# Earlier loads for attention, and a shorter selection for one tile, in a one-core streaming step

## The chip, the cores and the metric

One core of a Trainium2 chip runs the whole kernel as one launch. The metric is the time of an execution on the device, in microseconds; less is better. The engines are TensorE (PE; its weight loads are shown as PEld), VectorE (DVE), ScalarE (ACT), GpSimd (POOL) and SyncE (SP), which here only issues DMAs.

## The reference, cut to what matters

A layer takes 1024 prompt tokens, 64 sample tokens and 16 meta tokens of width 1024. After a norm one projection gives queries, keys, values and gates. Two mixers run beside each other: A is a sliding window with a sink in its softmax, B attends to the best 256 keys of an indexer's scores. Their gated sum goes through w_o and an MLP.

```python
rel = relu(einsum('bqhd,bsd->bqhs', qi, ki))
score = einsum('bqh,bqhs->bqs', wi, rel) * INDEX_SCALE
score = where(admissible[None], score, -inf)
top_val, top_idx = lax.top_k(score, n_sel)          # n_sel = 256
...
s = where(valid, s - slopes * dist, -inf)           # B, over the keys kept
p = softmax(concatenate([s, sm], -1)); out = p @ v  # sm: scores of the meta keys
...
mix = (sigmoid(g_a) * o_a + sigmoid(g_b) * o_b) @ w_o
```

## The kernel before

Everything is float32; each product is made from a rounded part ("hi") and a remainder ("lo"). The kernel is a row of blocks. Inside a block each engine runs its own list of instructions, tied by semaphores; a block ends when all engines have ended theirs, and only then does the next begin. DMAs are issued in program order by the engine whose list they stand in.

**projection** goes through the columns of w_in in chunks 1 to 9 (chunk 0 is done with the norm). Chunks 1 to 5 give queries, feature-major in 12 groups; 6 to 9 give gates, in 9 groups of token tiles (the last of 64 rows). A group is 24 matmuls in one PSUM bank (L894). ScalarE evacuates it to `stage` (`evacuate`, L635), SyncE stores it (`store`, L523; three stage slots). Between the groups of chunks 1 to 5, 7 and 8, TensorE makes the index scores of one of seven tiles, ScalarE their relu and weighting (L672, L676), GpSimd the sum over heads (`add_head`, L740), and VectorE selects (L865, L869): a round finds the eight largest of each row and overwrites them with TAKEN, 32 rounds for 256 keys, two tiles interleaved. `finish` turns the scores into a mask of distances. The last tile in this order is tile 2, with 384 keys; its first 20 rounds run beside the last 20 of tile 3 with 512 keys.

In the last chunk, SyncE waits until all index scores are added and loads the attention keys in natural order, twice each (`load_keys`, 12 prompt DMAs, 16 for the sample part), then goes on with the stores. After groups 0 to 6 TensorE turns three key groups each (`turn_attention_keys`, L917; 21 in all, 11 of them of the prompt); ScalarE copies each twice (L654, L655), GpSimd makes the lo parts (`keys_lo`, L759). When TensorE has ended its last group, GpSimd zeroes the sink rows and sets the ones columns of the values (L775, L778), and SyncE loads the first section's queries (L600), all values (L607) and stores the last four masks (L545), then waits for its stores, and the block ends. The raw keys, the index keys and the projection's weights lie where values, queries and keys are put later, which is why such loads wait.

**attention** has 18 sections: tiles 7 to 0 and then the sample tile, branch A and then B of each. A section has 16 units (two halves, 8 pairs of heads; 8 for the sample). A unit is `score` (L1504), `subtract_distance` on VectorE (L1439), `exp` on ScalarE (L1397), `turn` (L1518), copies (L1391, L1451), `weigh_values` (L1534). Section 0's queries are split by ScalarE (L1405) and VectorE (L1472) at the block's start, all later ones by GpSimd, one section ahead (`split_queries`, L1346, L1349). SyncE's list is: load_q(1), wait for the masks, distances, gates, copies to the outputs, then the loads and stores of each section. After attention come w_o with the norms, and the MLP.

## Time and profile before

| | us |
|---|---|
| runs, median of 3 (lowest to highest) | 2042.55 (2040.95 to 2051.41) |
| the profiled execution, its own time | 2042.43 |
| its span, first to last instruction | 2040.6 |
| TensorE matmul busy (share) | 1924.3 (94%) |
| VectorE busy | 1178.2 (58%) |
| ScalarE busy | 713.2 (35%) |
| GpSimd busy | 578.8 (28%) |

Times in the rows are from the start of the span. Chunk 9 of the projection runs from 521 to 587 us, attention from 613.6 to about 1070 us. PEclk is the granted clock as a share of 2.4 GHz, so 0.50 is 1.2 GHz. "Idle before" is the time in which the engine stood, and the arrow says for whom.

### The profile page before, as it was taken

What the parts mean: (1) busy time and instruction counts of PE and PEld (TensorE: products, weight loads), DVE (VectorE), ACT (ScalarE), POOL (GpSimd) and SP (SyncE); (2) the same over time, 40 slices, a digit from 0 to 9 for tenths busy, and PEclk for the clock granted to TensorE, in tenths of its full rate; (3) what the DMA queues carried; (4) which work ended last, traced back from release to release, by engine and by line L of the source; (5) the groups of instructions that cost most, each with busy time, mean ns of one, the idle gap of its engine ahead of it and who ended that gap; (6) DMA issues with size and microseconds to landing.
All of it is one profiled execution on the core that took longest, in us unless ns stands there. A gap on an engine that the chain in (4) does not pass through costs nothing. (4 is left out here: it accounts for less than half of the span.)

```text
span 2040.6 us, 31131 instructions
## 1 busy us (share of the span) xinstructions
PE 1924.3 (94%) x11132; PEld 1734.4 (85%) x11132; DVE 1178.2 (58%) x2701; ACT 713.2 (35%) x1421; POOL 578.8 (28%) x444
## 2 busy tenths in 40 slices
PE   5989999999849999999997989999999999999995
PEld 5879999877638999999996868888888888888884
DVE  5249999998746566666754653333333333333337
ACT  4335544233215555655544332112122121212122
POOL 2315554133213232445611002222222222222224
PEclk9999999999977999999978999999999999999998
DMA  5423333332349134444613312111111111111104
GB/s 166 130 71 85 93 95 88 94 106 80 81 92 185 39 70 89 95 92 93 122 38 115 138 57 93 42 41 41 41 46 41 42 45 41 46 41 46 54 8 154
DMA packets 147465, 160.18 MB, mean 78 GB/s; under 512 B 35776, under 2 KB 115504, under 8 KB 147360
## 3 DMA queue, kind: packets, MB, share of 16 engines
q1 hardware_dynamic: 136416, 141.10, 26.0%
q10 hardware_dynamic: 10944, 17.72, 3.7%
q8 instruction: 62, 1.02, 0.2%
q14 instruction: 43, 0.35, 0.1%
HBM read 120.63 MB, written 39.27 MB: 78 GB/s over the span
## 5 line engine op out<-in xcount | busy, mean ns | idle before, releaser
L2042 PE MATMUL ps<-x2T_hi,weights 128*128 128x362 f32 (+1 forms) x1536 | 383.8, 329 | 5.3 <-DVE weights L2008 5.3
L2060 PE MATMUL ps<-weights,hid_hi 128*128 128x512 f32 (+1 forms) x1152 | 363.0, 396 | 0.0
L2042 PEld LDWEIGHTS ps<-x2T_hi,weights 128*128 128x128 f32 x1536 | 273.9, 189 | 7.0 <-DVE weights L2008 5.5
L1993 DVE TENSOR_TENSOR total<-total,ps 128x512 f32<-128x512 f32 (+1 forms) x270 | 184.9, 687 | 164.2 <-PE ps L2060 163.3
L2060 PEld LDWEIGHTS ps<-weights,hid_hi 128*128 128x128 f32 (+1 forms) x1152 | 209.6, 182 | 57.1
L2042 PE MATMUL ps<-x2T_lo,weights 128*128 128x362 f32 (+1 forms) x768 | 253.1, 330 | 0.0
L1978 DVE TENSOR_TENSOR hidden<-hidden 128x362 f32<-128x362 f32 (+1 forms) x96 | 51.6, 537 | 311.6 <-ACT hidden L1951 311.6
L2060 PE MATMUL ps<-weights,hid_lo 128*128 128x512 f32 (+1 forms) x576 | 228.1, 396 | 0.0
L869 DVE MATCH_REPLACE8 score<-top,score 128x1024 f32<-128x1024 f32 (+6 forms) x224 | 207.2, 930 | 0.0
L865 DVE MAX8 top<-score 128x8 f32<-128x1024 f32 (+6 forms) x224 | 203.1, 937 | 1.9
L1911 POOL TENSOR_TENSOR weights<-down_raw,weights 128x512 fp32r<-128x512 f32 x64 | 83.0, 1296 | 419.6 <-ACT weights L1942 419.6
L1397 ACT ACTIVATE probs<-probs,neg 128x209 f32<-128x209 f32 (+19 forms) x272 | 168.9, 622 | 12.7 <-DVE neg L1439 10.7
L1534 PE MATMUL ps<-v_b_p,pt 128*128 128x65 f32 (+2 forms) x1280 | 172.7, 278 | 0.0
L1391 ACT ACTIVATE pt<-ps 128x512 f32<-128x512 f32 (+3 forms) x224 | 104.7, 490 | 194.1 <-PE ps L1518 193.8
L1534 PEld LDWEIGHTS ps<-v_b_p,pt 128*128 128x128 f32 (+2 forms) x1280 | 166.4, 195 | 5.7
L1903 POOL TENSOR_TENSOR weights<-up_raw,weights 128x256 fp32r<-128x256 f32 x124 | 87.9, 749 | 289.8 <-ACT weights L1933 289.8
L1518 PE MATMUL ps<-ident,probs 128*128 128x128 f32 (+2 forms) x976 | 164.1, 287 | 0.6 <-ACT probs L1397 0.6
L894 PE MATMUL ps<-xT_hi,w_hi 128*128 128x362 f32 (+1 forms) x480 | 159.4, 332 | 1.6 <-PEq L160 1.6
L894 PE MATMUL ps<-xT_hi,w_lo 128*128 128x362 f32 (+1 forms) x480 | 158.2, 330 | 0.0
L894 PE MATMUL ps<-xT_lo,w_hi 128*128 128x362 f32 (+1 forms) x480 | 157.9, 329 | 0.0
L1942 ACT ACTIVATE weights<-down_raw 128x512 fp32r<-128x512 f32 x64 | 40.1, 626 | 317.6 <-PE ps L2060 317.5
L1951 ACT ACTIVATE hidden<-ps 128x362 f32<-128x362 f32 (+1 forms) x96 | 45.5, 474 | 288.4 <-PE ps L2042 288.4
(188 smaller groups left out, 3618.6 us busy)
## 6 DMA issues: line engine op xcount, KB each, us to landing
w_raw<-in_w_in ACTq DMA_DIRECT2D x64, 256.0 KB, 3.0
up_raw<-in_w_up SPq DMA_DIRECT2D x64, 256.0 KB, 2.8
down_raw<-in_w_down SPq DMA_DIRECT2D x64, 256.0 KB, 2.6
q_raw<-q_scr SPq DMA_DIRECT2D x30, 512.0 KB, 8.1
gates<-gate_scr SPq DMA_DIRECT2D x34, 256.0 KB, 4.7
x_in<-in_x_prompt SPq DMA_DIRECT2D x16, 512.0 KB, 4.7
gate_scr<-stage SPq DMA_DIRECT2D x32, 256.0 KB, 3.1
q_scr<-stage SPq DMA_DIRECT2D x40, 181.0 KB, 3.0
```

Of the source, the lines that this page charges most:

```text
L865: dve.max(top8[:tile_rows(INDEX_TILES[i]), i % 2], works[i]).then_inc(select_step[i % 2], 1)
L869: dve.match_replace(works[i], top8[:tile_rows(INDEX_TILES[i]), i % 2], works[i], TAKEN)\
L894: last = pe.matmul(out, a, b, start=(k == 0 and j == 0), stop=(k == KT - 1 and j == 2))
L1391: act.activation(pt[:, u % PT, a:a + n, :], src, ACT.Copy).then_inc(copied_act, 1)
L1397: act.activation(probs[:, u % 3, 0:w], probs[:, u % 3, 0:w], ACT.Exp, bias=neg[:, branch, h:h + 1], scale=-1.0).then_inc(exped, 1)
L1518: last = pe.transpose(ps[0:rows, T_BANK + x % 3, b * P:(b + 1) * P], probs[:, u % 3, col:col + rows], c["ident"][:])
L1534: last = pe.matmul(out_bank(q)[:, a, :], pt[0:rows, u % PT, j, :], values(u, j, rows), start=(j == 0), stop=(j == len(tiles) - 1))
L1903: pool.tensor_tensor(up_lo[:, k, :], up_raw[:, k // 2, k % 2, :], up_hi[:, k, :].bitcast(F32), ALU.subtract).then_inc(up_lo_done, 1)
L1911: pool.tensor_tensor(down_lo[at], down_raw[:, u, :], down_hi[at].bitcast(F32), ALU.subtract).then_inc(down_lo_done, 1)
L1993: dve.tensor_tensor(out, out, ps[:r, UP_BANKS + g % DOWN_BANKS, :], ALU.add).then_inc(added, 1)
L2042: last = pe.matmul(ps[:, g % UP_BANKS, 0:n], a[:, k, fs], b, start=(k == 0 and i == 0), stop=(k == KT - 1 and i == 2))
L2060: last = pe.matmul(ps[:r, UP_BANKS + g % DOWN_BANKS, :], a, b[:, f, cols], start=(f == 0 and i == 0), stop=(f == FT - 1 and i == 2))
```

## The change

- **Last chunk, loads.** SyncE loads only the prompt's keys (`load_prompt_keys`, 9 DMAs; the meta rows are written twice by one DMA) and behind them the first section's queries (`load_first_queries`, 2 DMAs). The sample part moves to ScalarE's queue behind its evacuation of group 0 (`load_sample_keys`, 10 DMAs).
- **Last chunk, keys.** TensorE turns none after group 0, four key groups after each of groups 1 to 5 and the last after group 6.
- **Values.** Only branch A's prompt values are loaded in the last chunk, in two parts after the stores of groups 6 and 7, once GpSimd has zeroed their sink rows, for which it waits until all keys are turned. The meta rows of blocks three apart are one DMA, so 15 DMAs stand for 26. Branch B's values are loaded in the attention block and waited for at section 1, the sample's at the sample tile; the fills for them move there too.
- **First queries.** They get a place of their own (`q_st_first`); ScalarE rounds them after evacuating group 7, GpSimd subtracts at the end of its list. The splitting at the start of attention goes.
- **Masks.** The last four are stored at the start of attention, ahead of B's values; load_q(1) then waits until they have landed, since its buffer lies over theirs.
- **Selection of tile 2.** `by_removal`: 384 keys less 256 leaves 128, fewer than 256, so GpSimd sums the negated scores in reversed order of keys, VectorE finds the 128 largest in 16 rounds, and `finish` masks those taken instead of those not taken.
- **Places.** Weights, keys, queries and attention's buffers are laid out anew; `half_of` gives hi and lo parts of a chunk the same half.

```diff
-W_RAW_AT = FOOT + 4 * HALF + X_BYTES
+KEYS_FROM = FOOT + X_BYTES + 2 * HALF
+W_RAW_AT = FOOT + X_BYTES + 4 * HALF
+Q_RAW_AT = W_RAW_AT + 4 * RAW * 512
...
+    out = place(nc, *first, FOOT, ("xT_hi", [P, KT, N_TOK], F32R), ("xT_lo", [P, KT, N_TOK], F32R), ("w", [P, 4, KT, 512], F32R),
...
+    return place(nc, KEYS_FROM, *[(n + "_fp32", shape, F32) for n, shape in KEYS])
...
+    return place(nc, ("q_st_first", [P, 2, HEADS, CHUNK], F32R), ("v_a_p", [P, SAMPLE_BLOCK, 2, 2 * COL], F32),
+                 ("v_a_s", [P, 2, 2 * COL], F32), ("v_b_p", [P, 9, COL], F32), ("v_b_s", [P, 9, COL], F32),
+                 FOOT, ("wo_raw", [P, KT, D], F32), ("pt", [P, PT, 9, P], F32), ("probs", [P, 3, N_META + N_QUERY], F32),
+                 ("merged", [P, 2, D // 2], F32),
+                 FOOT + X_BYTES, ("gates", [P, 2, 2, D // 2], F32), ("mixed", [P, 2, 2, D // 2], F32),
+                 ("q_st3", [P, 2, 2, HEADS, CHUNK], F32R), KEYS_FROM, *[(n, shape, F32R) for n, shape in KEYS],
+                 Q_RAW_AT, ("q_raw3", [P, 2, HEADS, P], F32), ("dist_b", [P, 2, N_META + N_QUERY], F32),
+                 ("neg", [P, 2, 2 * PAIRS], F32), ("neg_part", [P, 2, 2], F32), ("inv", [P, 2, QUAD], F32))
...
+    ROWS, ONES = sink_rows(kv, sample=False), ones_columns(kv, "v_a_p")
+    A_VALUES = banded_values(kv, t_scr)
+    q_first, q_first_hi = sem("p3_q_first"), sem("p3_q_first_hi")
+    FIRST_QUERIES = split_places(kv["q_st_first"], kv["q_raw3"][:, 0], 2)
+    VALUES_AT = 6
+    REVERSED_AT = 512
+    KEY_COLS = [slice(T_KA, T_KA + HD), slice(T_KA + HD, T_KA + 2 * HD), slice(T_KB, T_KB + HD)]
...
-        return range(min(3 * g, len(GROUPS)), min(3 * g + 3, len(GROUPS)))
-
+        first = max(0, 4 * (g - 1))
+        return range(min(first, len(GROUPS)), min(4 * g, len(GROUPS)))
...
+    def by_removal(i):
+
+
+        return keys_seen(INDEX_TILES[i]) - TOPK < TOPK
+
+    def work_place(i):
+        at = REVERSED_AT if by_removal(i) else N_META
+        return score[:tile_rows(INDEX_TILES[i]), mask_slot(i + 2), at:at + keys_seen(INDEX_TILES[i])]
...
-            def load_keys():
-                new, meta = slice(N_PROMPT, N_QUERY), slice(N_QUERY, N_TOK)
-                cols = [slice(T_KA, T_KA + HD), slice(T_KA + HD, T_KA + 2 * HD), slice(T_KB, T_KB + HD)]
...
+            def load_prompt_keys():
+                for i, cols in enumerate(KEY_COLS):
+                    src = t_scr[0:N_PROMPT, cols].rearrange("(j p) d -> p j d", p=P)
+                    for half in range(2):
+                        sp.dma_start(raw["raw_p"][:, :, i, half], src).then_inc(prompt_loaded, 16)
+                    src = t_scr[N_QUERY:N_TOK, cols]
+                    sp.dma_start(raw["raw_m"][:, i], src.unsqueeze(1).to_broadcast([N_META, 2, HD])).then_inc(prompt_loaded, 16)
+
+            def load_first_queries():
+                t = ATTENTION_ORDER[0]
+                src = q_scr[0:D, t * P:(t + 1) * P].rearrange("(h d) n -> d h n", d=HD)
                 for half in range(2):
-                    for i in range(3):
-                        sp.dma_start(raw["raw_p"][:, :, i, half, :], t_scr[0:N_PROMPT, cols[i]].rearrange("(j p) d -> p j d", p=P))\
-                          .then_inc(prompt_loaded, 16)
-                        sp.dma_start(raw["raw_m"][:, i, half, :], t_scr[meta, cols[i]]).then_inc(prompt_loaded, 16)
-                for half in range(2):
-                    for i in range(3):
-                        sp.dma_start(raw["raw_n"][:, i, half, :], t_scr[new, cols[i]]).then_inc(sample_loaded, 16)
-                        sp.dma_start(raw["raw_cm"][:, i, half, :], cache_meta[0, 0, :, (0, 1, 4)[i], :]).then_inc(sample_loaded, 16)
-                    sp.dma_start(raw["raw_ca"][:, :, half, :], cache_k_a[0, 0]).then_inc(sample_loaded, 16)
-                    sp.dma_start(raw["raw_cb"][:, :, half, :], cache_k_b[0, 0, :, 0, :].rearrange("(j p) d -> p j d", p=P))\
-                      .then_inc(sample_loaded, 16)
+                    sp.dma_start(kv["q_raw3"][half * HD:(half + 1) * HD, 0], src).then_inc(q_first, 16)
+
+            def load_values(part):
+                for dst, src in A_VALUES[part::2]:
+                    sp.dma_start(dst, src).then_inc(values_loaded, 16)
 
...
             for ch in range(1, N_CH):
                 if ch == LAST:
                     sp.wait_ge(added, IDX_HEADS * len(INDEX_TILES))
-                    load_keys()
+                    load_prompt_keys()
+                    load_first_queries()
                 for g in range(len(groups_of(ch))):
                     store(ch, g)
+                    if ch == LAST and g == VALUES_AT:
+                        sp.wait_ge(value_rows_set, len(ROWS))
+                        load_values(0)
+                    if ch == LAST and g == VALUES_AT + 1:
+                        load_values(1)
                     if ch == INDEX_CHUNK and g == 3:
                         for u in range(GROUP_BASE[ch] + 4 - STAGE, GROUP_BASE[ch] + 4):
...
                     store_mask(i + 2, INDEX_TILES[i])
-            def load_first_queries(heads, loaded):
-                t = ATTENTION_ORDER[0]
-                src = q_scr[heads.start * HD:heads.stop * HD, t * P:(t + 1) * P].rearrange("(h d) n -> d h n", d=HD)
-                for half in range(2):
-                    sp.dma_start(kv["q_raw3"][half * HD:(half + 1) * HD, 0, heads, :], src).then_inc(loaded, 16)
-
-            sp.wait_ge(group_done, GROUP_BASE[N_CH])
-            for piece in range(2):
-                load_first_queries(slice(8 * piece, 8 * piece + 8), kv["q_first"][piece])
-            sp.wait_ge(value_rows_set, VALUE_SETS)
-            for dst, src in value_loads(kv, t_scr, cache_v_a, cache_v_b, cache_meta):
-                sp.dma_start(dst, src).then_inc(values_loaded, 16)
-            for i in LATE_MASKS:
-                store_mask(i + 2, INDEX_TILES[i])
             all_stored(N_CH - 1)
...
                 hi.then_inc(kt_hi_done, 1)
                 as_is.then_inc(kt_raw_done, 1)
 
+            def load_sample_keys():
+                act.wait_ge(added, IDX_HEADS * len(INDEX_TILES))
+                for i, cols in enumerate(KEY_COLS):
+                    src = t_scr[N_PROMPT:N_QUERY, cols]
+                    act.dma_start(raw["raw_n"][:, i], src.unsqueeze(1).to_broadcast([N_SAMPLE, 2, HD])).then_inc(sample_loaded, 16)
+                    src = cache_meta[0, 0, :, (0, 1, 4)[i], :]
+                    act.dma_start(raw["raw_cm"][:, i], src.unsqueeze(1).to_broadcast([N_META, 2, HD])).then_inc(sample_loaded, 16)
+                for half in range(2):
+                    act.dma_start(raw["raw_ca"][:, :, half], cache_k_a[0, 0]).then_inc(sample_loaded, 16)
+                    act.dma_start(raw["raw_cb"][:, :, half], cache_k_b[0, 0, :, 0, :].rearrange("(j p) d -> p j d", p=P))\
+                       .then_inc(sample_loaded, 16)
+
+            def first_queries_hi():
+                act.wait_ge(q_first, 32)
+                act.wait_ge(kt_turned, PROMPT_GROUPS)
+                st, loaded = FIRST_QUERIES(slice(0, P))
+                act.activation(st, loaded, ACT.Copy).then_inc(q_first_hi, 1)
+
             def queries_hi(i):
                 r = tile_rows(INDEX_TILES[i])
                 act.wait_ge(q_loaded, 32 * (i + 1))
...
+                    if ch == LAST and g == 0:
+                        load_sample_keys()
                     if ch == LAST:
                         for j in key_groups_at(g):
                             copy_keys(j)
+                    if ch == LAST and g == VALUES_AT + 1:
+                        first_queries_hi()
                     if ch == INDEX_CHUNK and g == QUERIES_AT:
                         queries_hi(0)
...
-                out = score[:r, mask_slot(i + 2), N_META:N_META + n]
-                if h == 0:
+                out = work_place(i)
+                if h:
+                    pool.wait_ge(added, v)
+                else:
                     slot_free(pool, i + 2)
+                if by_removal(i):
+                    back = rel[:r, v % 2, n - 1::-1]
+                    if h == 0:
+                        pool.tensor_scalar(out, back, -1.0, None, ALU.mult).then_inc(added, 1)
+                    else:
+                        pool.tensor_tensor(out, out, back, ALU.subtract).then_inc(added, 1)
+                elif h == 0:
                     pool.tensor_copy(out, rel[:r, v % 2, 0:n]).then_inc(added, 1)
                 else:
-                    pool.wait_ge(added, v)
                     pool.tensor_tensor(out, out, rel[:r, v % 2, 0:n], ALU.add).then_inc(added, 1)
...
             pool.wait_ge(kt_lo_done, 3)
+            pool.wait_ge(kt_lo_done, 3)
+            pool.wait_ge(kt_turned, len(GROUPS))
+            for rows in ROWS:
+                pool.memset(rows, 0.0).then_inc(value_rows_set, 1)
+            pool.wait_ge(value_rows_set, len(ROWS))
+            for col in ONES:
...
             pool.wait_ge(kt_lo_done, 6)
-            pool.wait_ge(group_done, GROUP_BASE[N_CH])
-            for rows in sink_rows(kv):
-                pool.memset(rows, 0.0).then_inc(value_rows_set, 1)
-            pool.wait_ge(value_rows_set, len(sink_rows(kv)))
-            for col in ones_columns(kv):
-                pool.memset(col, 1.0).then_inc(value_rows_set, 1)
+            pool.wait_ge(q_first_hi, 1)
+            st, loaded = FIRST_QUERIES(slice(HD, P))
...
-                    dve.memset(score[0:CHUNK, slot, N_META + n - CHUNK:N_META + n], UNSEEN).then_inc(select_step[i % 2], 1)
+                    if by_removal(i):
+                        dve.memset(score[0:CHUNK, slot, REVERSED_AT:REVERSED_AT + CHUNK], -UNSEEN).then_inc(select_step[i % 2], 1)
+                    else:
+                        dve.memset(score[0:CHUNK, slot, N_META + n - CHUNK:N_META + n], UNSEEN).then_inc(select_step[i % 2], 1)
...
-                dve.tensor_scalar(work, work, TAKEN, -FAR, ALU.not_equal, ALU.mult).then_inc(select_step[i % 2], 1)
+                mask = score[:r, mask_slot(i + 2), N_META:N_META + n]
+                if by_removal(i):
+                    dve.tensor_scalar(mask, work[:, n - 1::-1], TAKEN, -FAR, ALU.is_equal, ALU.mult).then_inc(select_step[i % 2], 1)
+                else:
+                    dve.tensor_scalar(mask, work, TAKEN, -FAR, ALU.not_equal, ALU.mult).then_inc(select_step[i % 2], 1)
...
+            rounds = [(keys_seen(t) - TOPK if by_removal(i) else TOPK) // 8 for i, t in enumerate(INDEX_TILES)]
+            first = [0, rounds[0], rounds[0] + 12]
...
-                pe.wait_ge(sample_loaded if group.sample else prompt_loaded, 16 * (16 if group.sample else 12))
+                pe.wait_ge(sample_loaded if group.sample else prompt_loaded, 16 * (10 if group.sample else 9))
...
+def split_places(st, loaded, blocks):
+
+
+    return lambda rows: (st[rows, 0:blocks].rearrange("p e h n -> p h e n"),
+                         loaded[rows, :, 0:blocks * CHUNK].rearrange("p h (e n) -> p h e n", n=CHUNK))
+
+
+def banded_values(kv, t_scr):
+
+
+    va, out = kv["v_a_p"], []
+    cols_a, meta = slice(T_VA, T_VA + 2 * HD), slice(N_QUERY, N_TOK)
...
-        for i in range(blocks[1]):
-            tile, row = divmod(col, P)
-            out.append((va[row:row + N_META, blocks[0] + 3 * i, tile, VALUES], t_scr[meta, cols_a]))
+        (first, count), (tile, row) = blocks, divmod(col, P)
+        src = t_scr[meta, cols_a].unsqueeze(1).to_broadcast([N_META, count, 2 * HD])
+        out.append((va[row:row + N_META, first:first + 3 * count - 2:3, tile, VALUES], src))
...
+                for n in range(MASKS - SCORES, MASKS):
+                    t = INDEX_TILES[n - 2]
+                    w = N_META + keys_seen(t)
+                    sp.dma_start(dist_scr[t, 0:tile_rows(t), 0:w], kv["score"][:tile_rows(t), mask_slot(n), 0:w])\
+                      .then_inc(mask_stored[mask_slot(n)], 16)
+                for dst, src in B_VALUES:
+                    sp.dma_start(dst, src).then_inc(b_values_loaded, 16)
+                for n in range(MASKS - SCORES, MASKS):
+                    sp.wait_ge(mask_stored[mask_slot(n)], 16 * (n // SCORES + 1))
                 load_q(1)
-                for n in range(MASKS - SCORES, MASKS):
-                    sp.wait_ge(kv["mask_stored"][mask_slot(n)], 16 * (n // SCORES + 1))
                 for i in range(2):
                     load_dist(i)
                 for i in range(2):
                     load_gates(i)
+                sp.wait_ge(late_rows_set, len(LATE_SETS))
+                for dst, src in SAMPLE_VALUES:
+                    sp.dma_start(dst, src).then_inc(s_values_loaded, 16)
...
 
+                for n, (dst, value) in enumerate(LATE_SETS):
+                    if n:
+                        pool.wait_ge(late_rows_set, n)
+                    pool.memset(dst, value).then_inc(late_rows_set, 1)
...
-                        pe.wait_ge(kv["values_loaded"], 16 * VALUE_LOADS)
+                        pe.wait_ge(kv["values_loaded"], 16 * A_VALUES)
+                    if u == SECTION_END[0]:
+                        pe.wait_ge(late_rows_set, len(LATE_SETS))
+                        pe.wait_ge(b_values_loaded, 16 * len(B_VALUES))
+                    if u == SAMPLE_FROM:
+                        pe.wait_ge(s_values_loaded, 16 * len(SAMPLE_VALUES))
                     if act_copies(GROUPS[u + 1]):
```

## Rows read from the trace of the kernel before

**Rows 1.** The page, part 2: granted TensorE clock in 40 slices of 51 us, in tenths.

```profile
PEclk9999999999977999999978999999999999999998
```

**Rows 2.** Waits from 515 to 640 us: waiter, released by, us in total, times, longest.

```profile
PE ps L1504 <- DVE q_st L1472: 29.7, 1, 29.7
...
PE ps L917 <- DMA raw_m<-t_scr: 6.8, 1, 6.8
```

**Rows 3.** Stretches: us, PE, PEld, DVE, ACT, POOL busy (x), PEclk, DMA share, GB/s.

```profile
534.50:537.40 2.90, 2.90 (x10) 2.36 (x9) 2.90 (x8) 1.60 (x4) 0.00 (x0) 0.51 0.29 66
...
615.90:638.50 22.60, 21.90 (x108) 21.65 (x109) 13.57 (x60) 10.19 (x24) 6.43 (x2) 0.50 0.91 186
...
900.00:1000.00 100.00, 100.00 (x845) 96.20 (x844) 72.73 (x285) 59.78 (x125) 48.53 (x24) 1.00 0.59 105
...
588.00:589.00 1.00, 0.00 (x0) 0.00 (x0) 0.00 (x0) 0.00 (x0) 0.94 (x4) 0.76 0.55 133
```

**Rows 4.** TensorE in time: start us, us, engine, line, op, out<-in, count, idle before.

```profile
526.09 0.40 PE L894 MATMUL ps<-w_hi,xT_lo 128*128 128x512 f32 x1
533.31 0.28 PE L917 MATMUL ps<-ident,raw_m 16*128 16x16 f32 x1 [6.83 <-DMA raw_m<-t_scr]
```

**Rows 5.** SyncE's DMA issues in time: start us, us, what, count.

```profile
523.34 0.36 SPq L565 DMA_DIRECT2D raw_p<-t_scr  x1
...
530.11 0.81 SPq L567 DMA_DIRECT2D raw_m<-t_scr  x1
...
586.92 0.63 SPq L523 DMA_DIRECT2D gate_scr<-stage  x1
587.60 2.66 SPq L600 DMA_DIRECT2D q_raw<-q_scr  x4
590.30 13.62 SPq L607 DMA_DIRECT2D v_a_p<-t_scr  x26
...
610.62 2.42 SPq L545 DMA_DIRECT2D dist_scr<-score  x4
613.59 1.42 SPq L1266 DMA_DIRECT2D q_raw<-q_scr  x2
```

**Rows 6.** DMA issues from 515 to 640 us: count, KB each, median us to landing.

```profile
q_raw<-q_scr SPq DMA_DIRECT2D x5, 512.0 KB, 7.7
...
q_raw<-q_scr SPq DMA_DIRECT2D x4, 256.0 KB, 5.0
...
gate_scr<-stage SPq DMA_DIRECT2D x2, 128.0 KB, 2.4
...
dist_scr<-score SPq DMA_DIRECT2D x1, 200.0 KB, 3.1
```

**Rows 7.** ScalarE and GpSimd in time, around the seam.

```profile
580.77 0.60 ACT L635 ACTIVATE stage<-ps 128x512 f32<-128x512 f32 x1 [4.04 <-PE ps L894]
586.31 0.59 ACT L635 ACTIVATE stage<-ps 64x512 f32<-64x512 f32 x1 [4.94 <-PE ps L894]
...
613.60 2.00 ACT L1405 ACTIVATE q_st<-q_raw 128x1024 fp32r<-128x1024 f32 x2 [26.70 <-PEq L511]
...
586.40 2.32 POOL L775 MEMSET v_a_p<- 32x128 f32 x3 [5.51 <-PE ps L894]
...
622.15 1.89 POOL L1346 CAST q_st<-q_raw 128x2048 fp32r<-128x2048 f32 x1 [32.88 <-DMA q_raw<-q_scr]
624.12 4.54 POOL L1349 TENSOR_TENSOR q_st<-q_raw,q_st 64x2048 fp32r<-64x2048 f32 x1
```

**Rows 8.** TensorE's score matmuls in time: section 0's first, section 1's first, two in section 2.

```profile
615.97 1.61 PE L1504 MATMUL ps<-k_a_p,q_st 128*128 128x208 f32 x6 [29.69 <-DVE q_st L1472]
...
638.57 1.66 PE L1504 MATMUL ps<-k_b_p,q_st 128*128 128x488 f32 x4
...
704.63 0.46 PE L1504 MATMUL ps<-k_a_p,q_st 128*128 128x208 f32 x2
...
713.27 0.46 PE L1504 MATMUL ps<-k_a_p,q_st 128*128 128x208 f32 x2
```

**Rows 9.** VectorE in time: the last rounds of the selection.

```profile
569.24 0.56 DVE L865 MAX8 top<-score 128x8 f32<-128x384 f32 x1
...
584.24 0.36 DVE L843 TENSOR_SCALAR score<-score 128x384 f32<-128x384 f32 x1
584.64 0.56 DVE L847 TENSOR_TENSOR score<-score,dist 128x384 f32<-128x384 f32 x1
```

135 lines of the change are left out of this document (57 added, 78 removed).

## The prediction

> **What bounds the kernel now.** I read the page's clock line first, then who TensorE waited for, then stretches of time around the two long waits, and last the queues of SyncE and of the other engines there. TensorE is busy nearly everywhere and the granted clock is full for most of the span [rows 1]; what is left are holes. The list of waits names the largest: 29.7 us at L1504 for the first queries, and 6.8 us at L917 for the prompt keys' meta rows [rows 2]. Both lie at the seam between projection and attention. The stretches [rows 3] show what the holes cost besides themselves: after the first the clock is at 1.2 GHz (0.51) while chunk 9 restarts; after the second it is at 1.2 GHz for the whole first section of attention, 615.9 to 638.5 us, although TensorE is busy for 21.9 of these 22.6 us. From 640 to 1000 us TensorE never idles and has the full clock (the last 100 of these are in [rows 3]; the stretches before read alike), so a microsecond gained ahead of section 1 (the second section, tile 7 branch B) is a microsecond of the end; nothing behind it has an absolute time.
>
> The first hole: SyncE begins to load keys at 523.34, when the index scores are added, and issues twelve DMAs until 530.9 [rows 5]; TensorE has ended group 0 of chunk 9 at about 526.5 and stands until 533.31 [rows 4]. The second: TensorE's last group ends near 586.3. SyncE then issues the last gate store, 4 query loads, 37 value loads and 4 masks one after the other, from 586.92 to 613.04, and the next block opens at 613.59 [rows 5]. Then come the rounding and subtraction of the queries before TensorE starts at 615.97 [rows 7, 8]. So the issue of 45 small DMAs is the bound of that hole, not their bytes.
>
> **Part 1, keys a group later, fewer DMAs.** SyncE issues 9 prompt DMAs instead of 12, without the 12 short raw_n/raw_cm and 4 raw_ca/raw_cb loads behind them (they go to ScalarE's queue as 10). TensorE turns no key after group 0 but does group 1 first. A group is 24 matmuls or 5.54 us (the last two evacuations start 5.54 us apart, 580.77 and 586.31, [rows 7]), so the keys are wanted at 532.0 instead of 526.5. Old landing: 533.3. New: twelve issues took 7.6 us (523.34 to 530.92, [rows 5]), 0.63 each, so the ninth begins near 528.4, and with the old issue-to-landing of 3.2 us (533.31 less 530.11, [rows 4, 5]) that is 531.6 if issue is the limit. The same bytes must come, though: if the DMA engines are the limit, only the issue of later loads goes away, and 533.3 stays. So the remaining stall is 0 to 1.3 us; I take 0.3, nearer the issue limit. The removed idle is 6.83 us [rows 4]; the work from 533.31 to 537.4 at half clock would shrink by between 1.3 us (if transposes gain little) and half of 4.1, which is 2.05; I take 1.6. Sum: -6.8 - 1.6 + 0.3 = -8.1 us; the last evacuation starts at 578.2 instead of 586.3. The ScalarE issues (10 at the same 0.63 us, from 527.1 to about 533.4) come ahead of its copies of groups 0 to 3; TensorE wants these copies back only at group 2's end, 539, with some 2 us to spare.
>
> **Part 2, the shorter selection.** Alone, this is needed for part 1 to count. VectorE now ends at 585.2, just ahead of TensorE; twelve rounds of the 384-key tile run alone from 569.24 to 584.24, 1.25 us each [rows 9]. With 16 rounds instead of 32, started at the same time, these twelve vanish (-15.0 us) and four of the shared rounds lose this tile's half (about -0.9 us each, -3.6; an estimate from the same 1.25 less the idle that the other tile's instructions then no longer fill). VectorE ends near 567. Without it the block could not end before 585.2, and some 4 us of the gain would stay behind. It buys nothing more. GpSimd's eight additions read backwards: forwards they take 1.0 us and wait 4 us each for ScalarE; no row shows a backward read. Below: no gain, as they are covered by that wait; above: twice the time, which puts the last one, the keys' gate, 1 us later. I take 0 and keep 1 us.
>
> **Part 3, the block's end.** After group 6 the last key is turned (near 567); GpSimd sets the zero rows, 2.32 us [rows 7]; SyncE issues 8 value loads at 13.62/26 = 0.52 us [rows 5], ending near 573.4, the store of group 7, then 7 loads, ending near 577.7. That is ahead of the last evacuation's end (578.8). The merged meta copies make 15 of 26. The last store is issued at 578.8 and lands about 2.4 us later [rows 6], at 581.2; with the 0.55 us between blocks (613.04 to 613.59) attention opens at 581.75. ScalarE rounds the first queries behind evacuation 7, 2.0 us, and GpSimd subtracts in 4.54 us [rows 7], from near 575.3 to 579.8: hidden by 1.4 us. If that cover is gone, each microsecond counts whole. TensorE starts at once, since the 2.4 us of rounding and subtraction in the block are gone: 581.9 instead of 615.97. That is -34.1 us so far: 8.1 from part 1, 26.0 from here.
>
> **Part 4, section 0 and its successor.** What is late next is load_q(1). It now sits behind 4 mask stores (2.42 us), 4 value loads (2.1 us) and the wait for the masks' landing (3.1 us after the last issue), since its buffer shares their place: it is issued at about +5.0 and +5.7 us from the block's opening instead of +0. With 7.7 us to landing [rows 6] it is there at +13.4; with 5 us (four 256 KB query loads took that, [rows 6]) at +10.7. GpSimd's cast and subtraction, 1.89 + 4.54 us [rows 7], end at +17.2 to +20. Section 1 is wanted at +0.15 + 22.6 us if section 0 runs as slowly as now [rows 8]: covered by 3 us. The distances, issued until +9 and landing within 9 us, are covered too. So whether section 0 is faster decides. The hole is now 578.2 to 581.9, 3.7 us. In the present trace the clock fell 2.2 us after the last matmul (the stretch from 588 to 589 us averages 0.76, [rows 3]), so a hole of 3.7 us probably takes it down again, and section 0's own work did not bring it back in 22.6 us. I take 22.6 unchanged.
>
> The Trainium skill (TensorE: Matmul & The Clock Gate, "What's actually happening") says that the throttle is the default state and that recent activity of TensorE releases it. By that rule a section that keeps TensorE busy would soon run at full clock; this trace speaks against it for this work, since 21.9 busy microseconds of 22.6 left it at half.
>
> **Sum.** The profiled execution took 2042.43 us (2.0 us around its span of 2040.6), and the median of the runs is 2042.55, the same. Parts 1 and 3 give -34.1; part 2 and part 4 nothing. 2042.4 - 34.1 = 2008.3; I say 2008.
>
> **Rivals.** (a) The clock survives the short hole, chance 0.12. Units of section 0 then come every 0.864 us (ten from 704.63 to 713.27, [rows 8]), the section would be done at +13.5, and load_q(1) becomes the bound, at +17.2 to +20: 2.8 to 5.6 us less, of which a new idle of some 5 us gives back 1 in a cold start. 2003 to 2006. (b) The seam has a new last one: prompt keys still at 533.3 or later, with the clock dropped again (2 to 6 us), or GpSimd's chain, or SyncE's 15 value loads, running past the last store. For: three covers of 1 to 2 us each in a row. Against: each is made of durations shown. Chance 0.22, 2010 to 2016. (c) The value loads or queries are needed sooner than they land, so that the hole moves into attention: load_q(1) later than +22.6. It would take 3 us more than the 7.7 us of landing; the queue is emptier than it was. Chance 0.05, 2010 to 2014. (d) Slower than before: GpSimd reads backwards far slower. In chunk 8 it has per head 5.5 us less 1.3 (w_lo) less 1.0, so 3.2 us of room; beyond it each head holds up ScalarE's next relu and TensorE's index scores. Eight heads must lose over 34 us in all, thus an addition of about 8.5 us instead of 1.0, before the gain is gone. Nothing in the trace shows such a price. Chance 0.02, 2045. The forecast has the remaining 0.59.
>
> **Range.** Forecast alone: 2005 to 2011 (0.3 to 1.3 us of key stall, 1 us of backward reads, the phase at which the clock falls and rises, about 1.7 us each way). With (a) and most of (b): 2003 to 2015. A measurement of this kernel can tell about 0.5%, 10 us, from no change. Faster by more: every case but (d) and a far tail of (b) and (c), 0.96; within: 0.02; slower: 0.02.
>
> **What the new profile would show.** TensorE's wait at L917's successor is gone or under 1.5 us and no clock of 0.5 near 530; VectorE's last selection ends before 570; the hole at the seam is 3.5 to 4.5 us; the first value product does not wait for values; section 0 lasts 22 us at 0.50 (right) or 17 to 20 with a wait for q_st at its end (rival a); from section 1 on all lies 34 us earlier. I am wrong if the seam's last wait is GpSimd's or if the clock there is full.

## The result, and the profile after

The changed kernel took 2018.56 us, median of four runs (2012.18, 2018.38, 2018.73, 2020.75); the kernel before, timed beside it, took 2046.98 (2040.95, 2042.55, 2051.41, 2051.59; the median falls between two pairs). The ratio is 0.986, 95% interval 0.982 to 0.990. It is faster by more than the 0.5% that can be told, but 10 us slower than the 2008 that I predicted, and outside my range of 2003 to 2015. The profiled execution took 2018.38 us, span 2016.6.

The page's clock line of the changed kernel, which answers to [rows 1]. One slice at the seam still reads 7 (before, two slices did), and the dip at the end of attention, 7 and 8 from 1020 us before, now reads 6, 8 and 8 from 958 us:

```profile
PEclk9999999999979999999688989999999999999998
```

The waits of the changed kernel from 515 to 640 us, answering to [rows 2]: the wait of 29.7 us is 3.9 us for the block's opening, the wait for the keys 2.3:

```profile
PE ps L1577 <- PEq L530: 3.9, 1, 3.9
...
PE ps L970 <- DMA raw_m<-t_scr: 2.3, 1, 2.3
```

Stretches of the changed kernel (columns as in [rows 3]): group 1 and the wait for keys, the turning behind it, the seam, sections 0 and 1, then sections 13, 14, 15 and 16:

```profile
526.50:534.10 7.60, 5.30 (x24) 3.95 (x22) 7.60 (x22) 0.97 (x2) 0.00 (x0) 1.00 0.97 210
534.10:536.40 2.30, 2.30 (x15) 2.05 (x16) 2.30 (x7) 2.04 (x9) 0.00 (x0) 1.00 1.13 257
579.60:583.40 3.80, 0.00 (x0) 0.03 (x1) 0.00 (x1) 0.58 (x2) 1.86 (x2) 1.00 0.65 123
583.40:605.50 22.10, 21.28 (x108) 21.03 (x109) 12.52 (x59) 10.36 (x24) 7.01 (x7) 0.52 0.97 226
605.50:659.10 53.60, 53.60 (x419) 51.73 (x419) 34.54 (x101) 28.37 (x40) 11.75 (x6) 0.98 0.51 100
949.90:966.70 16.80, 16.80 (x146) 15.95 (x144) 12.65 (x51) 11.13 (x26) 9.43 (x5) 1.00 0.69 139
966.70:987.80 21.10, 21.01 (x118) 19.03 (x115) 12.52 (x65) 8.30 (x25) 12.01 (x8) 0.65 0.49 108
987.80:1011.20 23.40, 23.40 (x106) 20.91 (x105) 10.06 (x48) 7.97 (x24) 5.92 (x4) 0.50 0.22 45
```

The same three last sections in the kernel before, which no row ahead of the prediction shows (sections 13, 14, 15):

```profile
982.10:998.90 16.80, 16.80 (x145) 15.95 (x144) 12.57 (x51) 11.12 (x26) 9.70 (x5) 1.00 0.87 138
998.90:1013.90 15.00, 14.68 (x118) 13.27 (x115) 11.60 (x64) 8.09 (x25) 11.24 (x7) 1.00 0.28 66
1013.90:1033.80 19.90, 19.90 (x107) 17.92 (x105) 10.07 (x50) 8.19 (x25) 6.46 (x6) 0.62 0.58 117
```

The reader is to see two things. First, section 13 is alike to the tenth, and section 14 (tile 0, branch A) is not: 15.0 us at full clock before, 21.1 at 0.65 after, with the same 118 matmuls. Second, the time of the whole is made of these two places. Read by the start of each section:

| first score matmul of | before | after | moved |
|---|---|---|---|
| section 0 | 615.97 | 583.40 | -32.6 |
| section 1 | 638.57 | 605.54 | -33.0 |
| section 14 | 998.91 | 966.68 | -32.2 |
| section 15 | 1013.89 | 987.78 | -26.1 |
| section 16 | 1033.78 | 1011.23 | -22.6 |
| end of the span | 2040.6 | 2016.6 | -24.0 |

So 32 us of the promised 34.1 arrive at section 14. Then 9.6 us are given back in sections 14 and 15, whose work the change leaves as it was, and 1.4 us return behind attention. In the trace the half clock holds from 1018.6 for 30.7 us before, from 973.2 for 54.6 us after.

How the seam came about. SyncE's issues in the changed kernel, answering to [rows 5]:

```profile
523.10 0.99 SPq L583 DMA_DIRECT2D raw_p<-t_scr  x2
...
525.11 2.54 SPq L583 DMA_DIRECT2D raw_p<-t_scr  x2
...
529.69 1.52 SPq L585 DMA_DIRECT2D raw_m<-t_scr  x1
...
570.72 3.99 SPq L595 DMA_DIRECT2D v_a_p<-t_scr  x8
...
575.23 4.12 SPq L595 DMA_DIRECT2D v_a_p<-t_scr  x7
580.17 0.63 SPq L542 DMA_DIRECT2D gate_scr<-stage  x1
583.37 2.20 SPq L1363 DMA_DIRECT2D dist_scr<-score  x4
585.60 2.71 SPq L1366 DMA_DIRECT2D v_b_p<-t_scr  x4
588.87 1.31 SPq L1335 DMA_DIRECT2D q_raw<-q_scr  x2
```

TensorE at the three places of [rows 4, 8]:

```profile
534.10 0.23 PE L970 MATMUL ps<-ident,raw_m 16*128 16x16 f32 x1 [2.30 <-DMA raw_m<-t_scr]
...
583.40 0.97 PE L1577 MATMUL ps<-k_a_p,q_st_first 128*128 128x208 f32 x6 [3.88 <-PEq L530]
...
605.54 1.97 PE L1577 MATMUL ps<-k_b_p,q_st 128*128 128x488 f32 x4
```

GpSimd in the changed kernel, answering to [rows 7], with one of the additions of tile 2 that read backwards, and VectorE's last mask, answering to [rows 9]:

```profile
511.15 1.01 POOL L779 TENSOR_TENSOR score<-score,rel 128x384 f32<-128x384 f32 x1
...
576.84 4.58 POOL L825 TENSOR_TENSOR q_st_first<-q_raw,q_st_first 64x2048 fp32r<-64x2048 f32 x1 [1.93 <-ACT q_st_first L688]
...
596.39 1.89 POOL L1425 CAST q_st<-q_raw 128x2048 fp32r<-128x2048 f32 x1 [12.17 <-DMA q_raw<-q_scr]
598.36 4.53 POOL L1428 TENSOR_TENSOR q_st<-q_raw,q_st 64x2048 fp32r<-64x2048 f32 x1
```

```profile
566.48 0.69 DVE L900 TENSOR_TENSOR score<-score,dist 128x512 f32<-128x512 f32 x1
```

### The profile page after: what moved, and what is told of

Read it like the earlier page. It is cut to its first block and busy times, and to the rows that moved or that the text cites. A ratio compares the mean times of both kernels' runs of the same rounds, so it can differ in the third digit from the quotient of the medians.

```text
span 2016.6 us, 31063 instructions
## 1 busy us (share of the span) xinstructions
PE 1930.6 (96%) x11132; PEld 1740.3 (86%) x11132; DVE 1160.4 (58%) x2651; ACT 712.6 (35%) x1420; POOL 584.8 (29%) x445
## 5 line engine op out<-in xcount | busy, mean ns | idle before, releaser
L947 PE MATMUL ps<-xT_hi,w 128*128 128x362 f32 (+1 forms) x960 | 245.9, 330 | 1.6 <-PEq L160 1.6
L922 DVE MATCH_REPLACE8 score<-top,score 128x1024 f32<-128x1024 f32 (+5 forms) x208 | 199.2, 965 | 0.0
L918 DVE MAX8 top<-score 128x8 f32<-128x1024 f32 (+5 forms) x208 | 195.0, 971 | 1.6
L947 PE MATMUL ps<-w,xT_hi 128*128 128x512 f32 (+1 forms) x576 | 180.8, 395 | 0.0
L947 PEld LDWEIGHTS ps<-xT_hi,w 128*128 128x128 f32 x960 | 171.6, 189 | 2.5 <-POOL w L208 2.0
L947 PE MATMUL ps<-xT_lo,w 128*128 128x362 f32 (+1 forms) x480 | 157.7, 329 | 0.0
```

The costliest lines, as they stand in the source:

```text
L918: dve.max(top8[:tile_rows(INDEX_TILES[i]), i % 2], works[i]).then_inc(select_step[i % 2], 1)
L922: dve.match_replace(works[i], top8[:tile_rows(INDEX_TILES[i]), i % 2], works[i], TAKEN)\
L947: last = pe.matmul(out, a, b, start=(k == 0 and j == 0), stop=(k == KT - 1 and j == 2))
```

## Experiments

**Theories.** A: the change is worth what its seam shows, 32 to 33 us; the rest of the miss is the clock falling at another moment among the small sections 14 to 17, which changes from run to run in either kernel. B: the change itself makes those sections slower (other places in memory, loads moved into attention), so the loss belongs to it.

### Both kernels again

No edit. Kernel before:

> The kernel before, unchanged, timed five times more. Theory A (the clock in the last small sections of attention falls at a moment that differs from execution to execution, in either kernel): the times spread over 5 to 10 us, and within the kernel the longer ones have the lower mean granted clock; in its profile, TensorE's scores of section 1 begin near 638.6 us as before, but the fall of the clock after 900 us need not be at 1018.6. Theory B (the new kernel's layout or loads make the clock fall earlier): the old kernel falls at about 1018 us every time, and its times lie within 0.3%.

Twelve runs: three at 2041.40 to 2042.46 and nine at 2049.77 to 2054.29, nothing between (ratio 1.002, 1.000 to 1.004). The runs of the kernel before beside it lie the same way, 12 of 23 at 2040 to 2043 and 11 at 2051 to 2054. This profile, of 2053.16 us, is one of the long ones; its sections 13 and 14:

```profile
981.90:998.70 16.80, 16.80 (x145) 15.95 (x144) 12.55 (x51) 11.10 (x26) 9.71 (x5) 1.00 0.91 149
998.70:1022.50 23.80, 23.80 (x118) 21.64 (x115) 12.68 (x65) 8.21 (x25) 11.72 (x8) 0.56 0.57 115
```

Up to 998.7 it is the profile before to 0.3 us; then section 14 takes 23.8 us instead of 15.0, because the half clock begins at 1001.4 (61.4 us long) instead of 1018.6 (30.7). The same program thus has two lengths 10 us apart, by when the clock falls; the three shorter runs have a mean granted clock of 0.964 to 0.965, the nine longer ones 0.957 to 0.959. I call them short and long runs. That shows A's mechanism without any change, and the profile that I had taken my sum from was one of the short kind.

> The changed kernel, unchanged. Theory A: times spread from about 2008 to 2021 us; where the clock falls as late as the old kernel's did, the time is near 2009; all spans up to section 14 (tile 0, branch A) repeat within 1 us of 966.7 for its first score. Theory B: it falls near 974 us every time and all times lie near 2018.

2012.35, and five of 2017.41 to 2020.84; ratio 0.986 (0.983 to 0.989). The profile repeats the one above: section 0 at 582.98, section 14 from 966.28 to 987.32, half clock from 972.9 for 54.6 us. Of ten runs of the changed kernel two are short (2012.2 and 2012.4), eight long.

### The selection alone

On the kernel before: `by_removal`, `work_place`, the reversed sums and 16 rounds for tile 2, with nothing else of the change.

```diff
...
-            ROUNDS = TOPK // 8
+            rounds = [(keys_seen(t) - TOPK if by_removal(i) else TOPK) // 8 for i, t in enumerate(INDEX_TILES)]
...
```

> The kernel before with the shorter selection of tile 2 alone. My account: nothing waits for VectorE there, so section 0 still starts at 616.0 +- 0.3 us and section 1 at 638.6; VectorE's last mask ends near 567 instead of 585.2. The rival (VectorE did hold the block's end, or the reversed reads on GpSimd cost) would move section 0's start: earlier by up to 1 us, or later by 1 us or more.

Ten runs of 2049.43 to 2052.84; ratio 1.002 (1.000 to 1.004). VectorE's last mask ends at 568.3 instead of 585.2, and TensorE's waits are what they were:

```profile
PE ps L1528 <- DVE q_st L1496: 29.7, 1, 29.7
PE ps L941 <- DMA raw_m<-t_scr: 7.1, 1, 7.1
```

The edit buys nothing alone, as I had it; section 0 began at 616.47 and section 1 at 639.07, 0.5 us later than in the kernel before, a little outside the 0.3 us that I allowed. Its sections 14 and 15 bear on theory B. The layout and the loads of this kernel are those of the kernel before, and yet the two sections are the changed kernel's, with the clock falling 6.5 us into section 14 and staying down for 54.6 us in both:

```profile
1000.20:1021.30 21.10, 21.02 (x117) 19.03 (x115) 12.49 (x65) 8.29 (x25) 11.69 (x8) 0.65 0.51 112
```

All ten runs are of the long kind, where 15 of 35 runs of the unchanged kernel on the same chip were short: an edit that touches nothing on the path may still weigh on which kind comes up.

### The change without the shorter selection

```diff
-        return keys_seen(INDEX_TILES[i]) - TOPK < TOPK
+        return False
```

> The changed kernel with 32 rounds for tile 2 again. My account: VectorE ends at about 585, so that the attention block opens at 585.5 to 586 instead of 583.4, section 0 starts 2 to 2.5 us later than in the changed kernel, and that is all the shorter selection is worth here. Rival: the selection carries much of the gain (10 us or more lost without it).

2007.90 to 2023.27, median 2020.03; ratio 0.988 (0.984 to 0.992). The profile, of the fastest run, shows what it holds back: VectorE ends at 584.58 and the block opens at 584.86 instead of 583.37, so 1.5 us, not the 4 that I had (nor the 2 to 2.5 expected here). In this run the clock happened to rise early in section 0, and TensorE then met the next limit:

```profile
584.90:603.90 19.00, 14.58 (x108) 14.03 (x108) 12.66 (x61) 10.90 (x24) 6.96 (x7) 0.85 0.95 235
```

```profile
PE ps L1577 <- POOL q_st L1428: 4.2, 1, 4.2
```

GpSimd's subtraction of section 1's queries ended at +19.0 us, and section 1 began there. This is my rival (a), by chance of the clock.

### The keys turned as before

```diff
-        first = max(0, 4 * (g - 1))
-        return range(min(first, len(GROUPS)), min(4 * g, len(GROUPS)))
+        return range(min(3 * g, len(GROUPS)), min(3 * g + 3, len(GROUPS)))
```

> The changed kernel, but three key groups turned after each of groups 0 to 6 as before, with the new loads. My account of part 1: the prompt keys land near 534 whoever waits, so TensorE now stands from 526.2 to 534 (about 7.8 us instead of 2.3), the clock falls in it and costs 1 to 2 us more, and section 0 starts 5.5 to 7.5 us later than the changed kernel's 583.4. Rival (the fewer DMAs did it, not the later turning): the hole stays near 2 us and section 0 starts within 1 us of 583.4.

2016.04 and three of 2024.93 to 2025.77; ratio 0.988 (0.984 to 0.992). The wait is back, and with it the half clock (530.3, 6.8 us), and section 0 begins at 590.41, 7.0 us later than with the change:

```profile
PE ps L969 <- DMA raw_m<-t_scr: 7.7, 1, 7.7
```

So turning a group later is worth 7.0 us of the 32.6. The keys land near 534 (533.73 and 534.10) whether TensorE waits from 526.05 or from 531.8, and they landed at 533.31 in the kernel before: nine DMAs instead of twelve, now with ten loads of the sample part beside them from ScalarE's queue, did not bring them earlier.

### A warm clock through the seam

Behind the last group stand 14 matmuls of 512 columns into a bank that nobody reads, on the changed kernel:

```diff
+            pe.wait_ge(kt_hi_done, len(GROUPS))
+            pe.wait_ge(kt_raw_done, len(GROUPS))
+            for _ in range(14):
+                pe.matmul(ps[:, 5, :], xT_hi[:, 0, 0:P], w_hi[:, half_of(LAST), 0, :], start=True, stop=True)
```

> The changed kernel with 14 matmuls of 512 columns behind the last group, into a bank that nobody reads, so that TensorE works through 3.2 of the 3.9 us hole. If the clock stays at full level, section 0 needs 13.5 us of work, GpSimd's subtraction for section 1 (done 19.5 us after the block's opening) becomes the bound, and section 1 starts near 603, 2.5 us earlier than the changed kernel's 605.5. If section 0's own work cannot hold the clock, it falls within the section and section 1 starts between 603 and 605.5.

Ratio 0.986 (0.983 to 0.990), as without it. The clock held through the seam, and section 0, which began at 585.04 instead of 583.40, was done 13 us after its start, but section 1 began at 604.78 instead of 605.54:

```profile
585.00:598.00 13.00, 12.06 (x108) 11.71 (x108) 11.64 (x59) 10.26 (x23) 0.63 (x5) 1.00 0.86 221
```

```profile
PE ps L1581 <- POOL q_st L1432: 6.6, 1, 6.6
```

During that wait of 6.6 us the clock fell (600.6, for 10.2 us), and section 1 took 55.3 us instead of 53.6. A fast section 0 is worth nothing while load_q(1) is late: the second half of rival (a), measured.

### load_q(1) earlier, then with the warm clock

Masks 5 and 6 are stored behind the store of group 1 of chunk 9, 7 and 8 behind that of group 6, and load_q(1) stands ahead of B's values:

```diff
+                    if ch == LAST and g == 1:
+                        store_mask(5, INDEX_TILES[3])
+                        store_mask(6, INDEX_TILES[4])
...
+                        sp.wait_ge(mask_ready, MASKS)
+                        store_mask(7, INDEX_TILES[5])
+                        store_mask(8, INDEX_TILES[6])
```

> The changed kernel with the last four masks stored in the last chunk, so that load_q(1) is the first DMA of attention. By my account load_q(1) is covered when section 0 runs at half clock: section 1 still starts near 605.5 us, and only GpSimd's subtraction ends some 5 us earlier, near 598. Rival: load_q(1) holds section 1 already, and section 1 starts earlier by 1 us or more.

2010.21 to 2018.86, median 2016.11; ratio 0.984 (0.981 to 0.988). Section 1 begins at 602.83, 2.7 us sooner and not near 605.5 as expected. That doesn't show that load_q(1) held it before: in this profile the clock fell at 586.25 for only 6.8 us, so that section 0 ran mostly at full clock and lasted 14.9 us. It began late, at 587.97: the wait for the keys was 2.8 us, and half clock from 535.05 for 6.8 us went with it.

> Both together: the 14 matmuls in the hole and the masks stored early. If the clock holds and load_q(1) was the only bound behind it, section 1 starts 14 to 15 us after section 0, near 598, 7 us earlier than the changed kernel; if it does not hold, near 605 as without.

Both edits together. 2001.99 to 2015.65, median 2013.16; ratio 0.982 (0.978 to 0.986). In the profile, of the fastest run, section 1 begins at 598.97, 6.6 us ahead of the changed kernel's, section 14 at 958.98, 7.7 ahead:

```profile
583.90:599.00 15.10, 12.26 (x109) 11.74 (x109) 12.58 (x61) 10.83 (x24) 7.04 (x7) 1.00 0.97 198
```

In this run the clock fell only at 977.27, in section 15, and section 14 took what it takes in the profile before, 15.0 us with 14.68 busy, though the places in memory and, but for the masks and load_q(1), the loads are those of the changed kernel:

```profile
959.00:974.00 15.00, 14.68 (x118) 13.27 (x115) 11.63 (x64) 8.09 (x25) 11.53 (x7) 1.00 0.27 62
```

With the selection-only run this is the plainest evidence against B: section 14 has the short form in the new layout and the long form in the old one. The profiles without the shorter selection (965.39 to 980.37) and of the keys turned from group 2 on (963.35 to 978.33) have the short form too.

### Work that holds the clock in the last sections

On this last variant, in sections 14 to 16, one extra matmul of 252 columns per unit (then two), whose result is never read:

```diff
+                    if ALL[u][0] in range(14, 17):
+                        for _ in range(1):
+                            pe.matmul(ps[:, O_BANK + q % 2, QUAD * COL:512], kv["k_b_p"][:, 0, 0:P], kv["k_b_p"][:, 0, 0:512 - QUAD * COL],
+                                      start=True, stop=True)
```

> The kernel with masks early and the seam filled (the one with 14 matmuls), and in sections 14 to 16 (tile 0 and the sample's branch A, 40 units) one more matmul of 252 columns ahead of each unit's value products, into unused columns of the output bank. If TensorE's sparse work in the small sections lets the clock fall, more work there holds it longer: the half-clock stretch that starts between 973 and 983 us gets shorter or goes, and for 5 to 6 us of added work some 5 to 12 us come back; times near 2000 to 2008 with less spread. Rival (the fall has nothing to do with how dense the work is): the stretch stays 34 to 58 us and the time is about 5 to 9 us longer than without, as the additions run at half clock.

Five runs of 1990.65 to 1995.20 and one of 2020.45, median 1991.56; ratio 0.975 (0.970 to 0.979). More work, and 20 us less time by the medians (10 against the fastest run without it). The expectation was 2000 to 2008. Sections 14 and 15 of the profile:

```profile
960.00:976.10 16.10, 16.03 (x130) 14.65 (x127) 12.06 (x64) 8.23 (x25) 11.67 (x7) 1.00 0.32 74
976.10:991.40 15.30, 15.18 (x122) 13.74 (x121) 9.53 (x49) 7.92 (x25) 5.92 (x5) 1.00 0.66 140
```

> As the one before with two such matmuls per unit: 80 in all, 10 to 12 us of work at full clock. By the density account the half-clock stretch is gone in every execution and the sections 14 to 16 take their full-clock time plus 10 to 12 us: no faster than one matmul per unit, but the narrowest spread. Rival: longer by twice the amount of the one before, stretch unchanged.

Four runs of 1993.53 to 1997.04, median 1995.10; ratio 0.974 (0.971 to 0.976). No run fell back, as one had with a single matmul; the second matmul costs its own time, some 3.5 us.

### Tile 0 elsewhere, and the keys two groups later

Both on the kernel with masks early and a warm seam, without the work in the last sections. First the order of the tiles:

```diff
-ATTENTION_ORDER = list(range(SAMPLE_TILE - 1, -1, -1)) + [SAMPLE_TILE]
+ATTENTION_ORDER = [7, 0, 6, 1, 5, 2, 4, 3, SAMPLE_TILE]
```

> Masks early, seam filled, and the tiles of attention in the order 7, 0, 6, 1, 5, 2, 4, 3, sample. By the density account the clock still falls in tile 0's sections, now the third and fourth, but the dense sections of tile 6 bring it back, and tiles 3 and the sample at the end keep it longer: half-clock time in attention of 15 to 35 us in place of 34 to 58, total 2000 to 2010. Rival: the fall is tied to the end of attention (the stores and loads there), and comes at the same late place.

2006.92 to 2010.60, median 2008.06; ratio 0.980 (0.978 to 0.983). The half clock left the end of attention and came at 675.5, where tile 0 now lies, for 47.8 us. The fall follows the small tile; it isn't tied to a time. The sample's sections, now behind tile 3, kept the full clock. The half clock was not shorter, as I had expected (15 to 35 us).

Then the keys, turned after groups 2 to 6:

```diff
+        last = len(GROUPS) if g >= 6 else 4 * max(0, g - 1)
+        return range(4 * (g - 2), last) if 2 <= g <= 6 else range(0)
```

> Masks early, seam filled, and the keys turned after groups 2 to 6 (4, 4, 4, 4, 5) in place of 1 to 6. The 2.3 us stand for the prompt's keys goes, and with it the fall of the clock that followed it in some executions; the fifth group after group 6 waits up to 1 us for ScalarE's copy. Section 0 starts 1 to 2.5 us earlier relative to group 0 of chunk 9. Rival: the keys' copies and lo parts now end late enough to hold the block's end, and nothing is gained.

1998.72 to 2013.66, median 2006.17; ratio 0.979 (0.976 to 0.983). The wait for keys is gone and section 0 begins at 581.12, 2.8 us sooner than with masks early and warm seam alone; the clock fell in section 0 in spite of the extra matmuls (583.7, 20.5 us), so section 1 began at 602.68.

### Both kernels with the clock held

The two extra matmuls on the kernel before and on the changed kernel, meant to take the late clock out of both sides:

> The kernel before, with two extra matmuls of 252 columns ahead of each unit's value products in sections 14 to 16; their result is never read. If the late half clock is what parts the runs of the kernel before into two groups and takes from it what it gains at the seam, this stretch is gone and every run lies in one narrow group: 2053 less what it took away, as between the same pair on the last variant (2013.2 to 1995.1, 18 us, of it some 10 between the groups): 2027 to 2035. If the extra work helps only kernels whose seam is short, no change from 2041 to 2053.

Nine runs of 2035.78 to 2043.48 and one of 2056.08, median 2037.85, beside a kernel before at 2050.73 (2039.28 to 2054.14): a miss against the 2027 to 2035 expected. The profile, of 2043.06 us, shows that the matmuls did not prevent the fall in section 14 but brought the clock back for section 15:

```profile
998.80:1023.80 25.00, 25.00 (x142) 23.45 (x139) 12.63 (x65) 8.18 (x25) 11.48 (x7) 0.66 0.55 109
1023.80:1040.80 17.00, 17.00 (x139) 15.66 (x137) 9.88 (x49) 8.02 (x24) 6.01 (x5) 1.00 0.14 36
```

> The changed kernel with the same extra matmuls. Seam theory (the change itself is worth what its profile shows ahead of section 1, 32 to 33 us, and the missing 9 us of the first comparison were the late clock alone): this run lies 32 to 34 us under the one of the kernel before with the same matmuls, 1994 to 2002. Rival (some part of the change costs time behind the seam, by its new places or the later loads in attention): the difference of the two stays at 24 to 29 us.

Four runs of 2003.26 to 2005.14, median 2004.09 (1994 to 2002 expected), with full clock throughout these sections:

```profile
965.60:982.80 17.20, 17.20 (x140) 15.92 (x139) 12.17 (x64) 8.20 (x25) 11.71 (x7) 1.00 0.36 81
```

Median against median the change is worth 33.8 us, with the three runs of the kernel before in which the clock seems to have fallen (2043.06, 2043.48, 2056.08; mean granted clock 0.968, 0.968 and 0.962 against 0.970 to 0.972) counted in. Without them the median before is 2036.23 and the difference 32.1; lowest against lowest it is 2035.78 - 2003.26 = 32.5, and at the start of section 14 (998.8 against 965.6) 33.2. That is A's 32 to 34; B's 24 to 29 is out.

### All together

The keys after groups 2 to 6, masks early, warm seam, one extra matmul.

> Everything that helped, together: keys turned after groups 2 to 6 (4, 4, 4, 4, 5), masks stored early, warming matmuls in the seam, and one extra matmul per unit in sections 14 to 16. If the gains add: 1991.6 less the 2.3 to 2.8 us that the earlier section 0 gave, 1988 to 1990. If the clock at the seam decides (it stayed down in section 0 with the keys so placed): 1991 to 1994.

1987.89, 1988.88, 1996.48, 2004.43, 2005.61, 2011.49; median 2000.45, ratio 0.977 (0.973 to 0.981), above both of the expected spans. The profiled run is the fastest of the study and has section 1 at 595.86 and full clock to 1034.7, so the gains add when the clock stays up; in four of six it evidently did not (mean granted clock 0.974 to 0.982 against 0.986 and 0.987), and no profile shows where. By its median the variant with one extra matmul and the keys as in the change, 1991.56, is the best kernel here, 27 us below the changed one; the two did not run side by side.

## Why the prediction was right or wrong

**The bound at the seam: right.** The two holes were the gain, and each shrank for the reason given.

**Part 1: right in kind, 1.1 us too much.** Predicted -8.1 with 0.3 us of stall left; the undoing measured 7.0, and the stall was 2.30. I had chosen "nearer the issue limit". The row of 526.5 to 534.1 shows the other limit: DMA engines 0.97 busy at 210 GB/s, and even the issues stretched (2.54 us for two, where 0.63 each was taken). That points at the bytes as the bound, as the other end of my own bracket said (533.3). But the queue was not the old one either: ten loads of the sample part were issued from ScalarE's queue from 526.28 on, beside the prompt's keys, and a `raw_p` load took 4.0 us from issue to landing where it had taken 3.1. No run separates the two. The cold 4 us behind the wait did vanish: 1.00 from 534.1.

**Part 2: right.** VectorE ends at 567.2 (predicted near 567), alone worth nothing, and the backward additions take 1.01 us. What would stay behind without it was 1.5 us, not 4: the block opened 1.6 us later than predicted, and without the edit it opened at 584.86, 0.9 us sooner than I had (585.2 plus 0.55).

**Part 3: right, but for part 1's term.** The value loads took 0.50 and 0.59 us each (0.52 predicted), the last evacuation ended at 580.15 (578.8 predicted), the block opened at 583.37 (581.75), and GpSimd's 4.58 us ended at 581.4, ahead of the block. TensorE began at 583.40 instead of 581.9: -32.6 instead of -34.1. Most of the missing 1.5 us had come in by the last evacuation, 1.35 us late, behind a key stall 2.0 us longer than predicted.

**Part 4: right.** Section 0 took 22.1 us at 0.52, and the queries of section 1 were ready at 602.9, +19.5 (predicted +17.2 to +20), a cover of 2.7 us (predicted 3). The clock fell at 584.07, 4.6 us after the last matmul, where my rows had 2.2 us. The first half of rival (a), a warm section 0 with load_q(1) as the next bound, came up once by itself and once forced: section 1 began 19.0 and 19.7 us after section 0 instead of 22.1, so 3.1 and 2.4 us less, the lower end of the 2.8 to 5.6 that I gave. At section 1 only 1.6 and 0.8 us of it were left, since section 0 began later in both kernels. Rivals (c) and (d) did not occur; (b)'s stall occurred without its clock drop.

**The sum: the step that failed.** I wrote that a microsecond gained ahead of section 1 "is a microsecond of the end; nothing behind it has an absolute time", and made the sum against one profiled execution as if its clock repeated. The 10.1 us between 2008.3 and 2018.4 are 1.5 at the seam, 0.3 up to section 14, and 8.2 behind it. Those 8.2 are the clock: the profile before had it fall at 1018.6, 4.7 us into section 15, the one after at 973.2, 6.5 us into section 14, and the kernel before does either by itself (first experiment) at a cost of 10 us. The new layout isn't the cause: section 14 took 15.0 us in it when the clock fell later, and 21.1 us in the old layout when it fell at the same point. Like against like, the medians of the long runs of both kernels are 2051.6 and 2018.6, 33 us apart. My median before (2042.55, three runs) and my profile were of the short kind; in the whole study 27 of 74 runs of the kernel before were, and two of ten of the changed kernel. The sign was safe, the range was not: it gave the phase of the clock 1.7 us each way, and needed 10.

What stood in my rows and was not used: the three runs of before were spread over 10 us (2040.95 to 2051.41), and I never asked which part of the trace could hold them. The clock line [rows 1] pointed at it: 7 and 8 from 1020 us on, at the end of attention, which I passed over as behind the change.

The Trainium skill (TensorE: Matmul & The Clock Gate, "What's actually happening") has it that recent activity of TensorE releases the throttle. The added matmuls agree with it: with one more of 252 columns per unit the clock, which fell without it, held in the profile and, by the times, in five of six runs. Busy time alone does not: section 15 of the changed kernel kept TensorE busy for 23.4 of 23.4 us and stayed at 0.50.

**Open.** What decides, run by run, at which moment of sections 14 and 15 the clock falls; why the short runs of the two kernels are only 29 us apart (2041.4 and 2012.3, the latter two runs, of which no profile was taken); and whether the change makes short runs rarer (two of ten against 27 of 74 is too few to say). The selection alone, with none in ten, hints that the timing of what lies ahead weighs on it. Nor is it shown what in the added matmuls holds the clock: they change the number of matmuls, their width and the share of transposes (29 of 118 matmuls in section 14) all at once.

## What to carry to other kernels

Before a sum is made against a median, look at the spread of the runs: two groups can mean, as here, that one stretch has two lengths, and two profiles of the same kernel show which; the forecast then needs both. A gain made early is a gain of the end only up to the first stretch whose clock is not settled. And where small matmuls keep TensorE busy yet at 1.2 GHz, a few useless wider ones can pay: here one per unit in three sections took some 20 us off the median.

## What the runs showed of the hardware

- The granted clock fell to 1.2 GHz, or stayed there, in stretches in which TensorE hardly idled (sections 14 and 15: 21.01 busy of 21.1 us, 23.4 of 23.4), all of matmuls of 208 columns and fewer. Section 12 of the same kernel, also of 208 columns and fewer, kept 2.4 GHz while busy for 17.00 of 17.00 us (first line below). So neither the busy share nor the width tells by itself. With one matmul of 252 columns more per unit the clock stayed at 2.4 GHz. At 1.2 GHz the width hardly counted up to 208 columns: 468 ns for 208 columns, 442 for 144, 442 and 397 for 65, in the rows below.

```profile
932.90:949.90 17.00, 17.00 (x150) 16.34 (x148) 13.69 (x62) 9.49 (x24) 10.56 (x7) 1.00 0.39 92
```

The changed kernel's matmuls at half clock, 973.3 to 1027.8 us, grouped by line and form (operand names, shapes, count, busy us, mean ns):

```profile
L1577 PE MATMUL ps<-k_a_s,q_st 128*128 128x208 f32 x16 | 5.9, 468 | 0.0
L1612 PE MATMUL ps<-v_b_p,pt 16*128 16x65 f32 x16 | 5.5, 442 | 0.0
...
L1577 PE MATMUL ps<-k_a_p,q_st 128*128 128x144 f32 x16 | 5.5, 442 | 0.0
...
L1612 PE MATMUL ps<-v_b_p,pt 128*128 128x65 f32 x16 | 4.7, 397 | 0.0
```

- The length of a wait did not by itself decide what the clock did. Waits of 2.30 us (changed kernel) and 2.61 us (one extra matmul) for the keys left it up; one of 2.44 us (two extra matmuls) went with half clock for 3.4 us, and one of 2.84 us (masks early) with half clock for 6.8 us.
- While the attention keys were loaded, in rows of 256 bytes and on two queues, the DMA engines moved 210 GB/s at a share of 0.97. Nine DMAs for the prompt's keys, with the ten others beside them, landed at 534.1, twelve for the same bytes at 533.3.
- GpSimd's addition (a subtraction in its place) with one operand read backwards took 1.01 us for 128x384; the addition forwards took 1.01 us in the kernel before.
